# The parts of w_ada in a buffer of their own, and another order for the opening and block 0

## The chip, the cores and the metric

The kernel runs on one core of a Trainium2 chip. The metric is the device time of one execution in microseconds (us). Its engines are named as in the profile: PE (TensorE, matrix products), PEld (PE's weight loads), DVE (VectorE), ACT (ScalarE), POOL (GpSimd) and SP (SyncE, which here only issues DMAs). A name with q behind it (SPq, ACTq, DVEq, POOLq) is an engine's instruction queue.

## What is computed

One decoder block in float32 on 2048 rows of 1024 columns:

```
mod = silu(c) @ w_ada + b_ada ; sh1, sc1, g1, sh2, sc2, g2 = split(mod, 6)      # each 1024 wide
h   = rmsnorm(x, norm1_g) * (1 + sc1) + sh1
u_conv, u_ssm, gl_conv, gl_ssm = split(h @ w_in)                                # 1024, 512, 1024, 1024
y_conv = silu(layernorm(depthwise_conv31(a * sigmoid(gate)))) @ conv_proj
y_ssm  = gelu(diagonal state space scan of u_ssm) @ ssm_glu, halves za * sigmoid(zb)
x   = x + g1 * ((sigmoid(gl_conv) * y_conv + sigmoid(gl_ssm) * y_ssm) @ w_out)
h   = rmsnorm(x, norm2_g) * (1 + sc2) + sh2
x   = x + g2 * ((silu(f_gate) * f_up) @ w_ffn_out) ;  out = rmsnorm(x, final_g)
```

## The kernel before

**Products.** Each float32 operand of a large product is split into a high part and a low part in the float32r format, and a product is three matmuls (high by high, high weight by low data, low weight by high data: lines 1488 to 1490, and 1633 to 1635 for w_out).

**Stages.** An opening makes sh1 and sc1, the normalized first rows and the tables of the state space. Then four blocks (`mixers(b)`, b = 0 to 3) of 512 rows each run the mixers up to `x + g1 * ...`. The feed-forward follows. The change touches the opening and the four blocks; the feed-forward has the same work as before.

**Weight chunks.** In a block PE goes through 48 weight chunks of 128 x 1024 values: 4 of w_in for the state space (`us0` to `us3`), 8 for the convolution's inputs (`ua`, `ug`, in pairs), 16 for the gates (`gl0` to `gl15`), 8 of ssm_glu, 4 of conv_proj, 8 of w_out. SP loads a chunk into a ring of three buffers `raw` (`load`, L1871), POOL rounds it into `w_hi` (L1782) and subtracts for `w_lo` (L1784), each in a ring of two (SPL = 2), and PE takes 24 matmuls of 512 columns from it. So POOL may start chunk w when PE is through with chunk w-2. Every matmul waits in program order; the order of each engine is written out by hand, and each step of an engine raises a counting semaphore (`Steps`) on which the others wait.

**Parts of w_ada.** g1, sh2, sc2 and g2 are made one in each block (`MADE`). POOL forms `acc` = sum over k of `cact[:, k] * w_ada[k]`, k = 0 to 7, plus b_ada / 128 as a ninth part: nine loads of 128 x 1024 that go through the same ring `raw`, one behind every third weight chunk (`MIX_CHUNKS`). Each is a scaling (TENSOR_SCALAR, in place, L1761, or into `acc` for the first, L1768) and an addition (L1764), both 128 x 1024 (`part_of_ada`). PE sums `acc` over the partitions in `modulation` behind `cp1`.

**Opening.** sh1 and sc1 (2048 columns of w_ada) are made by PE from eight slabs of 128 x (4 x 512) values, 1 MB each, loaded by SP into four buffers `ada` (L1839); PE takes four matmuls with 4-column weights from each (L1434), in the order of the slabs, and only after `zc`, which DVE writes after the transpose `v0` of the poles' rows `nat_a` (L1423). DVE then writes `modrow` (L623), PE turns it (`mt`), DVE writes `scale0`, ACT makes h in eight tiles (two operations each, L1027) and DVE their low parts (`h_split`, L534), one behind each of the eight turns of three operations that write `wm` (L632 to L634). DVE's arithmetic for the state space (L586 to L619) stands ahead of `modrow`.

**Block 0.** It has work that the others don't: PE's transposes of `wm` and `cx` (`state_matrix`, L1467 and L1473) behind `us3`, whose results ACT copies back and stores to `wt_scratch`; the rotation tables (DVE `kargs` L523 to L526, ACT L1065 and L1066); DVE's 27 operations for `vm` behind `gated(0, 0)`; PE's `kernel_tiles` (L1482) behind `ug3`. ACT issues eight DMAs that gather `u8` (L1117) behind `state_matrix`, then the tables, then the sigmoids of `ug0` to `ug3` (L1121). From there on all blocks do the same: PE's `S0` to `S3` (L1543) on `u8`, DVE's rotation and scan (L745 to L777), the gates on PE meanwhile, `Y0` to `Y3`, the rest of the convolution on DVE (L711, 97 operations in one run), `ys_lo` (L534), for which PE waits ahead of `za0`. DVE's L799 to L803 give the sum that PE's `ln1` (L1571) takes.

**Places in memory.** `g2b` (128 x 1024) is written only in block 3, when g2 is ready. `acc` isn't used before block 0.

Of the kernel before, what the change touches and what calls it, by code (L numbers as in the profile page):

```python
# [7 lines left out]
ALU = mybir.AluOpType  # L8
# [6 lines left out]
P = 128  # L15
# [30 lines left out]
def build(nc, x, c, w_ada, b_ada, norm1_g, w_in, conv_w, conv_b, conv_ln_g, conv_ln_b, conv_proj,  # L46
# [8 lines left out]
    NB = SEQ // TB  # L55
# [13 lines left out]
    ADA = 4  # L69
# [61 lines left out]
    with ExitStack() as ctx:  # L131
# [116 lines left out]
        def early(at, end, *buffers):  # L248
# [21 lines left out]
        cact = vt[:, 6 * KD:7 * KD]  # L270

# [49 lines left out]
        pe_pro = ["v1", "v0"] + [f"ada{n}" for n in R(len(SLABS))] + ["mt"] + h_steps + ["v2"]  # L321
# [150 lines left out]
        zeros_in, ada_scaled = sem("zeros_in"), sem("ada_scaled")  # L472
# [20 lines left out]
        def _(dve):  # L493
# [88 lines left out]
            norm_scale("pro")  # L582

# [10 lines left out]
            link(v.reciprocal(den, den))  # L594
            link(v.tensor_tensor(t0, nr, ar, ALU.mult))
# [6 lines left out]
            link(v.tensor_tensor(qi, qi, den, ALU.mult))  # L602

            def by_h(a):
# [10 lines left out]
                                        op0=ALU.mult, op1=ALU.add))  # L615
            link(v.tensor_copy(bank[4][:], flat2(b1)))
# [4 lines left out]

# [366 lines left out]
        def _(act):  # L988
# [114 lines left out]
            def mixers(b, next_x, row, which, last=False):  # L1103
# [9 lines left out]
                if b == 0:  # L1113
                    state_matrix()
# [904 lines left out]
```

## Time and profile before

| | us |
|---|---|
| median of 3 runs (lowest, highest) | 2761.34 (2752.03, 2761.76) |
| the profiled execution's own time | 2760.32 |
| its span, first to last instruction | 2758.5 |
| PE busy in the span | 2609.3 |
| POOL busy | 1852.2 |
| DVE busy | 1472.9 |
| ACT busy | 722.2 |

The mean granted clock of TensorE is 0.972 of full speed. Block 0 begins on PE at 64.07 us, block 3 ends and the feed-forward begins near 1380 us. Busy shares are averages over stages with different limits; what a stage is limited by is read from the waits in it. Idle time of an engine off the chain costs nothing.

### The profile page before, as it was taken

Reading aid. Unit: us, or ns where it says so; the run is one execution under the profiler, and the core shown is the slowest. Engines: PE = TensorE matmul, PEld = TensorE weight load, DVE = VectorE, ACT = ScalarE, POOL = GpSimd, SP = SyncE. Lnnn points to the kernel's source line nnn. Section 1 sums busy time; section 2 is a strip of 40 time slices with the busy share of each in tenths; the row PEclk is TensorE's granted clock in tenths of the full one; section 3 lists DMA queues with packets and bytes.
Section 4 is the critical chain, followed back from the end, with each engine's and each line's share of the span. In section 5 each row is a group of like instructions: output and inputs, shape, how many; then the busy total and the mean of one; then the engine's idle time right before and its main releaser. Section 6 shows DMA issues by size and latency. Waiting matters only on the chain.

```text
span 2758.5 us, 30542 instructions
## 1 busy us (share of the span) xinstructions
PE 2609.3 (95%) x11671; PEld 2136.7 (77%) x11671; DVE 1472.9 (53%) x1766; ACT 722.2 (26%) x1118; POOL 1852.2 (67%) x1134
## 2 busy tenths in 40 slices
PE   5889899899989999899989999999999999999998
PEld 2678687777877788787778888878888877888886
DVE  5599743966269562894653333473333334645531
ACT  3212321024201430024333234542333321211100
POOL 1767556876666767766587776788777755666664
PEclk9999998999989999899999999999999999999999
DMA  8686337562574527564232333222322336655532
GB/s 238 149 212 186 104 126 173 153 188 95 162 188 123 177 84 210 148 187 141 85 111 73 92 92 115 88 73 85 92 75 86 91 134 221 186 182 188 172 126 76
DMA packets 422906, 378.28 MB, mean 137 GB/s; under 512 B 95641, under 2 KB 333929, under 8 KB 422633
## 3 DMA queue, kind: packets, MB, share of 16 engines
q1 hardware_dynamic: 316256, 299.48, 36.0%
q10 hardware_dynamic: 106504, 76.85, 10.0%
q8 instruction: 93, 1.52, 0.2%
q14 instruction: 53, 0.43, 0.0%
HBM read 312.11 MB, written 55.71 MB: 133 GB/s over the span
## 4 chain that ended last, share of the span: by engine, by line
PE 76%; DVE 8%; POOL 8%; DMA 4%; issue 1%; ACT 1%; ACTq 1%; DVEq 0%; POOLq 0%
PE bank L1488 16%; PE bank L1490 16%; PE bank L1489 16%; PE bank L1716 5%; PE bank L1717 5%; PE bank L1718 5%; POOL w_lo L1784 3%; DVE bank L711 2%; PE bank L1633 2%; PE bank L1635 2%; PE bank L1634 2%; POOL raw L1761 2%; PE bank L1543 2%; POOL w_hi L1782 1%; POOL acc L1764 1%
## 5 line engine op out<-in xcount | busy, mean ns | idle before, releaser
L1782 POOL CAST w_hi<-raw 128x1024 fp32r<-128x1024 f32 x192 | 215.5, 1122 | 474.1 <-PE bank L1490 360.0
L1784 POOL TENSOR_TENSOR w_lo<-raw,w_hi 128x1024 fp32r<-128x1024 f32 x192 | 481.5, 2508 | 15.4
L1488 PE MATMUL bank<-h_hi,w_hi 128*128 128x512 f32 x896 | 367.3, 410 | 64.9 <-POOL w_lo L1784 60.4
L1489 PE MATMUL bank<-h_lo,w_hi 128*128 128x512 f32 x896 | 360.3, 402 | 0.0
L1490 PE MATMUL bank<-h_hi,w_lo 128*128 128x512 f32 x896 | 359.2, 401 | 0.0
L711 DVE SCALAR_TENSOR_TENSOR bank<-uc,cwt,bank 128x512 f32<-128x512 f32 x464 | 328.4, 751 | 8.0
L1802 POOL TENSOR_TENSOR fw_lo<-fsum,fw_hi 128x512 fp32r<-128x512 f32 x176 | 233.7, 1330 | 106.2 <-ACT fw_hi L1296 106.2
L1488 PE MATMUL bank<-xc_hi_T,fw_hi 128*128 128x512 f32 x704 | 276.6, 393 | 8.6 <-DVE tr L895 6.3
L1716 PE MATMUL bank<-ow_hi,hid_hi 128*128 128x512 f32 x704 | 274.7, 390 | 7.6 <-DVE hid_lo L955 7.6
L1489 PE MATMUL bank<-xc_lo_T,fw_hi 128*128 128x512 f32 x704 | 275.1, 391 | 0.0
L1490 PE MATMUL bank<-xc_hi_T,fw_lo 128*128 128x512 f32 x704 | 275.1, 391 | 0.0
L1717 PE MATMUL bank<-ow_hi,hid_lo 128*128 128x512 f32 x704 | 274.5, 390 | 0.0
L1718 PE MATMUL bank<-ow_lo,hid_hi 128*128 128x512 f32 x704 | 274.4, 390 | 0.0
L1488 PEld LDWEIGHTS bank<-h_hi,w_hi 128*128 128x128 f32 x896 | 175.6, 196 | 111.9 <-POOL w_lo L1784 70.2
L1488 PE MATMUL bank<-xc_hi_B,fw_hi 128*128 128x512 f32 x528 | 207.7, 393 | 4.7 <-issue 2.9
L1490 PE MATMUL bank<-xc_hi_B,fw_lo 128*128 128x512 f32 x528 | 206.7, 392 | 0.0
L1489 PE MATMUL bank<-xc_lo_B,fw_hi 128*128 128x512 f32 x528 | 206.7, 391 | 0.0
L1490 PEld LDWEIGHTS bank<-h_hi,w_lo 128*128 128x128 f32 x896 | 175.3, 196 | 38.7
L1489 PEld LDWEIGHTS bank<-h_lo,w_hi 128*128 128x128 f32 x896 | 176.1, 197 | 35.9
L1802 POOL TENSOR_TENSOR fw_lo<-raw,fw_hi 128x512 fp32r<-128x512 f32 x110 | 151.0, 1373 | 60.6 <-ACT fw_hi L1296 60.6
L955 DVE TENSOR_TENSOR hid_lo<-hraw,hid_hi 128x512 fp32r<-128x512 f32 x88 | 142.3, 1654 | 92.0 <-ACT hid_hi L1384 92.0
L1830 POOL TENSOR_TENSOR ow_lo<-raw,ow_hi 128x1024 fp32r<-128x1024 f32 x66 | 168.6, 2555 | 5.3
(292 smaller groups left out, 5038.8 us busy)
## 6 DMA issues: line engine op xcount, KB each, us to landing
raw<-in_w_in SPq DMA_DIRECT2D x112, 512.0 KB, 4.2
raw<-in_w_ffn_in SPq DMA_DIRECT2D x66, 512.0 KB, 5.3
raw<-in_w_ffn_out SPq DMA_DIRECT2D x66, 512.0 KB, 4.3
hid_scratch<-tr SPq DMA_DIRECT2D x88, 256.0 KB, 2.8
hraw<-hid_scratch SPq DMA_DIRECT2D x88, 256.0 KB, 3.7
raw<-in_w_ada SPq DMA_DIRECT2D x32, 512.0 KB, 4.0
ssm_m<-vk_scratch SPq DMA_DIRECT2D x32, 512.0 KB, 5.6
raw<-in_ssm_glu SPq DMA_DIRECT2D x32, 512.0 KB, 3.5
```

The costliest lines, as they stand in the source:

```text
L711: ins = v.scalar_tensor_tensor(out=dst, in0=src, scalar=w, in1=conv_bank(m)[:], op0=ALU.mult, op1=ALU.add)
L955: v.tensor_tensor(hid_lo[n % RING][:], hraw[n % 4][:], hid_hi[n % RING][:].bitcast(F32), ALU.subtract).then_inc(hid_lo_done, 1)
L1488: t.matmul(dst, wh, xh, start=first, stop=False)
L1489: t.matmul(dst, wh, xl, start=False, stop=False)
L1490: return t.matmul(dst, wl, xh, start=False, stop=last)
L1716: t.matmul(dst, hid_hi[hs][:, cols], ow_hi[slot][:, wcols], start=(k == 0), stop=False)
L1717: t.matmul(dst, hid_lo[hs][:, cols], ow_hi[slot][:, wcols], start=False, stop=False)
L1718: ins = t.matmul(dst, hid_hi[hs][:, cols], ow_lo[slot][:, wcols], start=False, stop=(k == KF - 1))
L1782: g.tensor_copy(hi[:], src[:]).then_inc(hi_done, 1)
L1784: g.tensor_tensor(lo[:], src[:], hi[:].bitcast(F32), ALU.subtract).then_inc(split_done, 1)
L1802: g.tensor_tensor(fw_lo[i][:], part[WEIGHTS[i]], fw_hi[i][:].bitcast(F32), ALU.subtract)\
L1830: g.tensor_tensor(lo[:], src[:], hi[:].bitcast(F32), ALU.subtract).then_inc(ow_lo_done, 1)
```

## The change

1. **Parts of w_ada, their own buffer.** They leave the ring `raw` (`MIX_CHUNKS` is gone) and go to `ada_part`, which is the memory of `g2b`. SP issues part k just ahead of weight chunk 4k+2 of the block, after the last piece of part k-1.
2. **Four pieces.** The scaling is a TENSOR_TENSOR with a broadcast factor on 128 x 512, twice, then the addition on 128 x 512, twice. Part k has its pieces behind chunks 4k+1, 4k+2 (scaling) and 4k+3, 4k+4 (addition); part 0 is scaled straight into `acc`. So a piece stands behind chunks 1, 2 and 5 to 36. PE's `modulation` waits for the counters of the pieces.
3. **Opening.** DVE sums slabs 0 and 1 into `acc` (eight operations on 128 x 512), PE takes slabs 2 and 3, then the poles' transpose, then slabs 4 to 7, then one matmul that adds DVE's sum. `zc` is written before the poles. The rows x are issued by ACT behind the poles and log_dt. SP's slabs 4 and 5 wait for DVE, 6 and 7 for PE. DVE writes `modrow`, `mod`, `scale0` and h's low parts ahead of its state space arithmetic and between its parts, and `wm` behind them.
4. **Block 0.** PE and ACT take `ua0` and `ug0` ahead of `state_matrix`; ACT issues the gather of `u8` and the sigmoid of `ug0` ahead of its copies for `state_matrix`.

The core of the diff:

```diff
-        if w % 3 == 2 and w // 3 <= KD:
-            MIX_CHUNKS.append(("ada", w // 3))
+    NA, ADA_EVERY = KD + 1, 4
+        ada_part = g2b
 # pe_steps, block 0
-                names += [f"wt{n}" for n in R(8)] + ["ct0", "ct1"] ... conv_in(0, 1, 2, 3) ...
+                names += conv_in(0) + [f"wt{n}" for n in R(8)] + ["ct0", "ct1"] + conv_in(1, 2, 3)
-        pe_pro = ["v1", "v0"] + [f"ada{n}" for n in R(len(SLABS))] + ["mt"] + h_steps + ["v2"]
+        pe_pro = ["v1"] + slabs(2, 4) + ["v0"] + slabs(4, 8) + ["ada0", "mt"] + h_steps + ["v2"]
 # DVE, opening
+            link(v.tensor_copy(zc[:, :, 3], cact), "zc")
+            sums = acc[:, 0:HALF]
+            for rows in R(2):
+                dve.wait_ge(ada_in[rows], 16)
+                for j in R(KD // 2):
+                    k = rows * KD // 2 + j
+                    if k == 0:
+                        link(v.tensor_scalar(sums, ada[rows][:, j, :], cact[:, k:k + 1], None, ALU.mult))
+                    else:
+                        link(v.scalar_tensor_tensor(out=sums, in0=ada[rows][:, j, :], scalar=cact[:, k:k + 1], in1=sums,
+                                                    op0=ALU.mult, op1=ALU.add), f"slab{rows}" if j == 3 else None)
             dve.wait_ge(*tensor.after("pro", "v0"))
...
             norm_scale("pro")
+            dve.wait_ge(*tensor.after("pro", "ada0"))
+            link(v.tensor_copy(modrow[:], bank[7][0:4, :]), "modrow")
...
+            scale_of(0)
+            for k in R(2):
+                h_split("pro", k)
...
+            dve.wait_ge(*scal.after(0, "wt7"))
 # ACT, block 0
-                if b == 0:
-                    state_matrix()
                 act.wait_ge(uz_out, 64 * (b + 1))
...
                 if b == 0:
+                    sigmoid_u(0)
+                    state_matrix()
                     rotation_tables()
-                    for m in R(KC):
+                    for m in R(1, KC):
                         sigmoid_u(m)
 # PE, opening
+            modulation_rows(2, 4)
             pe.wait_ge(poles_in, 64)
             turn_rows_in(0, nat_a, bank[0])
+            modulation_rows(4, 8)
+            pe.wait_ge(pro_v, mark["slab1"])
+            t.matmul(bank[7][0:4, :], one_of_4[:], acc[:, 0:HALF], start=False, stop=True)
 # POOL
+            def scale_part(b, k, half, done):
+                cols = slice(half * HALF, (half + 1) * HALF)
+                factor = (cact[:, k:k + 1] if k < KD else part128[:]).broadcast_to([P, HALF])
+                dst = ada_part if k else acc
+                if half == 0:
+                    pool.wait_ge(part_in, 16 * (NA * b + k + 1))
...
+                g.tensor_tensor(dst[:, cols], ada_part[:, cols], factor, ALU.mult).then_inc(done, 1)
+            def add_part(b, k, half, done):
...
+                g.tensor_tensor(acc[:, cols], acc[:, cols], ada_part[:, cols], ALU.add).then_inc(done, 1)
...
+                    k, turn = divmod(w - 1, ADA_EVERY)
+                    if 0 <= k < NA and turn < 2:
+                        scale_part(b, k, turn, part_scaled)
+                    if 0 < k < NA and turn >= 2:
+                        add_part(b, k, turn - 2, (part_half, part_done)[turn - 2])
 # SP
+            def load_part(b, k):
+                if k == 1:
+                    sp.wait_ge(part_scaled, 2 * (NA * b + 1))
+                elif b or k:
+                    sp.wait_ge(part_half, KD * b + max(k - 1, 0))
+                    sp.wait_ge(part_done, KD * b + max(k - 1, 0))
...
+                    if n % ADA_EVERY == 2 and n // ADA_EVERY < NA:
+                        load_part(b, n // ADA_EVERY)
                     load(b, n, key)
```

## Rows read from the trace of the kernel before

**Rows 1.** The page's part 4: the chain that ended last, shares by engine.
```profile
PE 76%; DVE 8%; POOL 8%; DMA 4%; issue 1%; ACT 1%; ACTq 1%; DVEq 0%; POOLq 0%
```
**Rows 2.** PE's waits for POOL in blocks 1, 2, 3: us, times, longest.
```profile
PE bank L1488 <- POOL w_lo L1784: 14.8, 5, 6.3
...
PE bank L1488 <- POOL w_lo L1784: 14.8, 5, 5.3
...
PE bank L1488 <- POOL w_lo L1784: 15.1, 6, 5.3
```
**Rows 3.** Timeline of PE in block 1: start us, us, instruction, idle before, releaser.
```profile
444.18 0.50 PE L1488 MATMUL bank<-h_hi,w_hi 128*128 128x512 f32 x1 [1.54 <-POOL w_lo L1784]
...
458.14 13.50 PE L1543 MATMUL bank<-u,ssm_m 128*128 128x64 f32 x64 [2.79 <-DMA u<-us_scratch]
...
501.71 0.80 PE L1488 MATMUL bank<-h_hi,w_hi 128*128 128x512 f32 x1 [6.28 <-POOL w_lo L1784]
...
524.22 0.80 PE L1488 MATMUL bank<-h_hi,w_hi 128*128 128x512 f32 x1 [3.71 <-POOL w_lo L1784]
```
**Rows 4.** Windows: length, busy (x) of PE PEld DVE ACT POOL, PEclk, DMA share, GB/s.
```profile
520.00:530.00 10.00, 6.29 (x17) 4.61 (x16) 9.61 (x13) 0.60 (x1) 7.45 (x5) 0.67 0.46 134
...
590.00:600.00 10.00, 8.40 (x38) 6.63 (x37) 9.87 (x10) 8.10 (x9) 7.71 (x5) 1.00 0.71 230
```
**Rows 5.** Timeline of POOL in block 1.
```profile
488.17 4.67 POOL L1761 TENSOR_SCALAR raw<-raw,vt 128x1024 f32<-128x1024 f32 x1
...
496.49 1.98 POOL L1782 CAST w_hi<-raw 128x1024 fp32r<-128x1024 f32 x1
498.55 3.10 POOL L1784 TENSOR_TENSOR w_lo<-raw,w_hi 128x1024 fp32r<-128x1024 f32 x1
...
580.04 1.04 POOL L1782 CAST w_hi<-raw 128x1024 fp32r<-128x1024 f32 x1 [1.91 <-PE bank L1490]
581.16 2.40 POOL L1784 TENSOR_TENSOR w_lo<-raw,w_hi 128x1024 fp32r<-128x1024 f32 x1
583.54 2.85 POOL L1761 TENSOR_SCALAR raw<-raw,vt 128x1024 f32<-128x1024 f32 x1
```
**Rows 6.** One line, a half-width sum of the feed-forward: duration in ns min/median/max, times.
```profile
L1798 POOL TENSOR_TENSOR fsum<-raw,raw x22: 1289/1298/3223, 1388.5 to 2207.2; 128x512 f32<-128x512 f32 x22
```
**Rows 7.** DVE's waits between 570 and 640 us (block 1).
```profile
DVE yc L809 <- PE bank L1571: 22.8, 1, 22.8
```
**Rows 8.** DMA to landing (us, min/median/max) of all loads into `raw`.
```profile
DMA to landing us min/median/max: 3.3/3.8/12.5
```
**Rows 9.** Timeline of the opening, PE and DVE.
```profile
18.16 0.36 PE L1423 MATMUL bank<-ident,nat_a 64*128 64x64 f32 x1 [9.64 <-DMA nat_a<-in_ssm_a_im]
...
19.11 28.91 PE L1434 MATMUL bank<-ada,zc 128*4 128x512 f32 x64 [0.59 <-DVE zc L571]
...
48.13 0.68 DVE L623 COPY modrow<-bank 4x512 f32<-4x512 f32 x1 [3.99 <-PE bank L1434]
```
**Rows 10.** Windows of the opening and block 0.
```profile
10.00:15.00 5.00, 0.00 (x0) 0.00 (x0) 0.00 (x0) 1.74 (x3) 0.00 (x0) 1.00 1.04 403
...
34.00:44.20 10.20, 10.20 (x25) 2.09 (x24) 9.26 (x22) 0.12 (x1) 2.63 (x2) 1.00 1.06 307
...
48.10:72.30 24.20, 13.97 (x58) 10.43 (x58) 22.67 (x37) 11.00 (x16) 0.85 (x1) 0.72 0.47 132
...
94.20:123.60 29.40, 27.69 (x141) 22.83 (x140) 0.00 (x0) 11.27 (x13) 20.50 (x11) 1.00 0.91 184
...
168.00:287.00 119.00, 105.06 (x507) 86.92 (x505) 117.02 (x137) 22.44 (x31) 89.56 (x42) 0.96 0.68 188
```
**Rows 11.** Timeline of block 0: ACT, its queue, and PE.
```profile
97.36 1.09 ACT L1108 ACTIVATE uz<-bank 128x512 f32<-128x512 f32 x1 [11.32 <-PE bank L1490]
...
104.37 13.25 ACTq L1117 DMA_DIRECT2D u<-us_scratch  x8
...
289.58 0.80 PE L1488 MATMUL bank<-ys_hi,w_hi 128*128 128x512 f32 x1 [6.46 <-DVE ys_lo L534]
```

More of the change, by code:

```diff
@@ L304, in pe_steps @@
             if b == 0:
-                names += conv_in(0, 1, 2, 3) + [f"kk{n}" for n in R(8)] + quarters
+                names += conv_in(0) + [f"wt{n}" for n in R(8)] + ["ct0", "ct1"] + conv_in(1, 2, 3)
+                names += [f"kk{n}" for n in R(8)] + quarters
             else:
@@ L327, in act_steps @@
             if b == 0:
-                names += [f"wt{n}" for n in R(8)] + ["sk", "ck"] + [f"ug{m}" for m in R(KC)]
+                names += ["ug0"] + [f"wt{n}" for n in R(8)] + ["sk", "ck"] + [f"ug{m}" for m in R(1, KC)]
                 names += [f"kk{n}" for n in R(8)] + [f"S{q}" for q in R(NQ)]
@@ L602, in _ @@
             link(v.tensor_tensor(qi, qi, den, ALU.mult))
+            h_split("pro", 3)
             def by_h(a):
@@ L1426, in _, with modulation_rows @@
             turn_rows_in(1, nat_v, bank[1])
+            pe.wait_ge(pro_v, mark["zc"])
+            def modulation_rows(lo, hi):
+                for n in R(lo, hi):
+                    kind, half, rows = SLABS[n]
+                    pe.wait_ge(ada_in[n % ADA], 16 * (n // ADA + 1))
+                    for j in R(KD // 2):
+                        k, r = rows * KD // 2 + j, 2 * kind + half
+                        ins = t.matmul(bank[7][0:4, :], zc[:, k, 3 - r:7 - r], ada[n % ADA][:, j, :],
+                                       start=(n == 2 and j == 0), stop=False)
+                    ins.then_inc(*tensor.step("pro", f"ada{n}"))
+            modulation_rows(2, 4)
             pe.wait_ge(poles_in, 64)
             turn_rows_in(0, nat_a, bank[0])
-            pe.wait_ge(pro_v, mark["zc"])
-            for n, (kind, half, rows) in enumerate(SLABS):
-                pe.wait_ge(ada_in[n % ADA], 16 * (n // ADA + 1))
-                for j in R(KD // 2):
-                    k, r = rows * KD // 2 + j, 2 * kind + half
-                    ins = t.matmul(bank[7][0:4, :], zc[:, k, 3 - r:7 - r], ada[n % ADA][:, j, :],
-                                   start=(r == 0 and k == 0), stop=(r == 3 and k == KD - 1))
-                ins.then_inc(*tensor.step("pro", f"ada{n}"))
+            modulation_rows(4, 8)
+            pe.wait_ge(pro_v, mark["slab1"])
+            t.matmul(bank[7][0:4, :], one_of_4[:], acc[:, 0:HALF], start=False, stop=True)\
+                .then_inc(*tensor.step("pro", "ada0"))
             pe.wait_ge(pro_v, mark["modrow"])
@@ L1780, in _ @@
                         pool.wait_ge(*chunk_used[b - 1][NW - SPL + w])
-                    src, hi, lo = raw[n % RAW], w_hi[w % SPL], w_lo[w % SPL]
+                    src, hi, lo = raw[w % RAW], w_hi[w % SPL], w_lo[w % SPL]
                     g.tensor_copy(hi[:], src[:]).then_inc(hi_done, 1)
```

103 lines of the change are left out of this document (48 added, 55 removed).

## The prediction

> **What bounds the kernel now.** I read the chain first: three quarters of the span are PE, so what counts is where PE waits [rows 1]. Then PE's waits by block: in blocks 1, 2 and 3 nearly all are for POOL's `w_lo`, 14.8, 14.8 and 15.1 us [rows 2]. Then when they fall: in block 1 one of 1.54 ahead of a DMA wait, one of 6.28 and one of 3.71 around 500 to 525 us, and the rest, 14.8 - 1.54 - 6.28 - 3.71 = 3.3, in two of some 1.6 near 592 and 610 [rows 2, 3]. Then the clock: it is at full speed through the 1.6 us waits, and at 0.67 in the 10 us that hold the 3.7 us wait [rows 4]; TensorE's levels are 1.2 and 2.4 GHz, so the long waits cost more than their own length. Last POOL beside it: in quiet stretches a cast and a subtraction take 1.12 + 2.38 = 3.50 us start to start and POOL then waits 1.91 for PE, so PE's pace is 5.4 per chunk; beside DVE's rotation and scan the same pair takes 2.06 + 3.1 = 5.1 [rows 5]. A part of w_ada is a scaling of 2.85 plus an addition of some 2.4, 5.3 in all: more than the 1.9 that POOL has to spare, so each one ends as a PE wait of about 5.3 - 1.9 - 1.9 = 1.5, the seen 1.6 [rows 5].
>
> In the opening the transpose of the poles waits 9.64 us for its DMA, the slabs' matmuls start only then, and run 28.91 us without a gap; DVE waits for them with `modrow` [rows 9]. The slabs' data come at 403 GB/s meanwhile [rows 10], so PE, started late, sets this stretch.
>
> **Parts in four pieces, quiet stretches.** A piece is a 128 x 512 TENSOR_TENSOR. Its nearest row is a half-width sum on POOL, 1.30 us [rows 6]. A broadcast operand is not in the trace. Lower bound: 1.2, half of the full-width 2.4 [rows 5]; upper: 2.3, half of the slowest scaling, 4.67 [rows 5]. I take 1.3. Chunk and piece are 3.5 + 1.3 = 4.8, under 5.4: 0.6 to spare, and PE's waits behind a part go to zero: 3.3 us in block 1, the same in block 2. In block 3, with long waits of 5.3 [rows 2] and, like block 1's second, some 3.5, 15.1 - 1.5 - 5.3 - 3.5 = 4.8.
>
> The 1.54 us wait goes too but brings nothing: the next thing PE does is wait 2.79 for the gather of `u8` [rows 3], whose start hangs on `us3`, not on what lies between; that wait becomes 4.3.
>
> At one place page and rows differ. POOL's two-input multiplication replaces a one-input one; the one-input scaling is 2.85 us, the two-input subtraction 2.40 [rows 5], so the exchange costs nothing here. The Trainium skill, GPSIMD Engine Reference, section "Elementwise - side-by-side cycle accounting", has it the other way: bodies held by one port at 1.03 cycles per element, two-input ones near 2.6, at 1.2 GHz 0.88 and 2.2 us for 1024 elements as an estimate. By that, scaling would get dearer by 1.3 us per part and the piece would be 1.1 us; POOL would still fit into PE's pace, so the sum is the same by both.
>
> **The same beside DVE.** From chunk 11 to chunk 15 of block 1 POOL works beside rotation and scan. Each of its operations is there some 0.8 longer than in quiet (1.98 against 1.04, 3.10 against 2.40, [rows 5]). A chunk with a piece is then 5.1 + 1.3 + 0.8 = 7.2 against PE's 5.4: POOL stays the bound, but evenly. Step by step: chunk 11 starts at 485.3 and its piece ends at 491.0; chunk 12 is ready at 496.1, 13 at 503.3, 14 at 510.5, 15 at 517.0. PE, at 5.4 each, would wait 0.6, 1.8, 1.8 and 1.0 = 5.2 instead of 6.28 + 3.71 = 10.0: 4.8 saved. The clock: the second long wait lost 10 x 0.33 = 3.3 us [rows 4], the first about as much; if waits under 2 us leave the clock up, as in the second row of [rows 4], up to 6.5 more. I take half, 3.2. So 8.0, and 8.0 + 3.3 = 11.3 per block; rounded 11, 11 and 8.0 + 4.8 = 12.5: **34.5 us in blocks 1 to 3**.
>
> What is late next there: `ys_lo`. DVE waits 22.8 for PE's `ln1` [rows 7], of which PE needs some 5.4 for `za0`, `za1`, so there is room for 17 us: enough. `modulation` moves from a sum finished behind chunk 26 to one behind chunk 36, the chunk of `cp0`, `cp1`: the last piece ends 1.3 us behind the split and PE still has 5.4 of matmuls in front: nothing.
>
> **Loads.** Part k is issued behind the last piece of part k-1 (behind chunk 4k) and is wanted behind chunk 4k+1: 5.4 - 1.3 = 4.1 us later; loads land in 3.8 (median), 3.3 at best [rows 8]. Behind it on SP stands raw chunk 4k+2, due at 5.4 + 1.9 = 7.3 behind chunk 4k's split, issued at 1.7 and landing, with the part ahead of it (0.5 MB at 403 GB/s is 1.3), at 1.7 + 3.8 + 1.3 = 6.8. Both fit by half a microsecond. A late part holds POOL's next cast; POOL is a ready chunk ahead (1.9 us), so up to 2.4 late costs PE nothing once, and later pieces give back 0.6 each. Zero; if each of seven tight parts cost 1 us, 7 x 4 = 28.
>
> **Opening.** `zc` is ready at about 11 instead of 19. Slabs arrive at 403 GB/s shared with the 2 MB of x: four slabs and x are 6.3 MB, 15.6 us plus 2 to start: slab 3 at 17.6, slab 2 near 14. A slab is 28.91 / 8 = 3.6 on PE [rows 9]. PE: 2 and 3 from 14 to 21.2, the poles 0.4, four more slabs 14.4 to 36.0, the added matmul 0.9: 37 instead of 48. **11 us.** DVE's eight operations (0.7 each, as the 32 of half width in a busy time of 22.67 [rows 10], 6 in all) end near 17, slab 5 is issued there, in time. `modrow` then starts a stretch that took 24.2 us to h's last low part, of which 24 turns of `wm` at 0.70 were 16.8 [rows 10]. These move behind, and the state space arithmetic, about 10.0 [rows 10], moves in; with some 2 us of waiting for ACT's first two tiles it is 7.4 + 10.0 + 2 = 19.4: **5 us more.** `us0` ends near 57 instead of 73, `us3`, without POOL's waits beside the tables (5.1 and 0.4), near 73.6; ACT took it up at 97.36 before [rows 11].
>
> **Block 0.** Then `ua0`, `ug0`, with POOL beside DVE's tables now, 12 us: 85.5. `state_matrix` comes next, but its copies stand on ACT behind the gather of `u8`: ACT has `us3` at 73.6, the store's landing at most 7.0 later [rows 11], eight issues of 13.25 in all [rows 11], a sigmoid with its table 2: 96. PE gets its two first banks in and then **waits some 9 us for ACT, a new wait**; `ua1` starts near 102. Before, it would be 104.4 + 10.9 = 115. Gain 13; 4 more if the issues take 9 with less traffic beside them. The part-wait of 2.6 us ahead of `kernel_tiles` goes: 15 to 16. DVE, idle for 29.4 us before `gated(0, 0)` [rows 10], has `vm` done by 124 and is not late for `kernel_tiles` at 135.
>
> From the rotation on, DVE is the bound of block 0: 117 of 119 us busy from 168 to 287 [rows 10], and PE waits 6.46 for its `ys_lo` [rows 11]. This run moves as a whole with PE's `S3`. What POOL's pieces save PE in the gates is given back at `za0`, where the wait grows from 6.5 to some 14. So block 0 with its opening brings **15 us**, not 16 + 8 + 8.
>
> **Sum.** 15 + 34.5 = 49.5. The profiled execution took 2760.3 (span 2758.5, 1.8 around it), 1.0 below the median of the runs, 2761.3: 2760.3 - 49.5 = 2711.
>
> **Rivals.**
> A. As worked out: 2711. Chance 0.45.
> B. The stretch beside DVE gives nothing: four short operations meet DVE four times where two did, 8.2 us per part (4 x 2.05) against 6.1 to 8.3 before, and waits near 2 us pull the clock down as the 3.7 did. For it: the 0.8 per operation. Against: they are spread over four chunks. Only 3.3 + 3.3 + 4.8 = 11.4 and the opening's 15 remain: 2734. Chance 0.22. The Trainium skill, SBUF - State Buffer, section "SBUF: two separate sides", calls the pair of ports that both share an exclusive lock, under which the loser "fully blocks": that speaks for this rival, and the lengthened rows agree.
> C. More: waits below 2 us leave the clock up (another 3 x 3.3), the issues of `u8` are short (4) and DVE's run, meeting shorter POOL operations, shrinks by 2: 2711 - 16 = 2695. Chance 0.23.
> D. The gain at the front is eaten by ACT's gather or by DVE's fixed run, blocks 1 to 3 as in A with late loads: 2760 - 3 - 25 = 2732. Chance 0.06.
> E. Slower: the multiplication with a broadcast factor is dear. Scaling and adding pieces of mean p cost nothing until p passes 1.9 us; from there each of the 34 chunks with a piece adds p - 1.9 in four blocks. With 4.67 for the scaling piece, the mean is 3.0 and 1.1 x 34 x 4 = 150, less the 50: 2860. For it: no row shows the form. Against: POOL's other forms lie within 1.2 to 1.4 per half. Chance 0.04, with all other ways that end without gain.
>
> A run can tell 0.5% (14 us) from no change. Faster by over 0.5% 0.94, within 0.5% 0.03, slower 0.03. For 8 in 10 the range reaches over B and C: 2690 to 2741.
>
> **What would show it.** Right: no wait of PE for POOL near the former 592 and 610; four or so short ones near 495 to 520 with the clock up; a POOL multiplication of 1.3 us; `modrow` near 37; a wait of PE for ACT's `wm` copies of some 9 us; a wait for `ys_lo` in block 0 of over 10. Wrong: POOL waiting for `ada_part`'s DMA; pieces over 1.9; DVE's run from rotation to `ys_lo` in blocks 1 to 3 ending behind the gates; `us3` later than 80.

## Result, and the profile after

The changed kernel takes 2682.9 us (median of 4 runs, 2677.2 to 2688.2), against 2761.6 for the kernel before on the same chip: a ratio of 0.972 (95% interval 0.969 to 0.975). That is 79 us saved where the prediction had 49.5 and a range of 2690 to 2741. The profiled execution took 2686.0 us, with a span of 2684.2.

I set the two traces side by side at one mark in each block: the first matmul of the output product that waits. In blocks 0 to 2 it waits for `m_lo`; in block 3 the product's only wait is one for `w_lo`, some 30 us further on in it, which makes that stretch longer by as much in both kernels. The marks lie at 363.87, 687.98, 1012.59 and 1373.07 us before, and at 351.26, 651.62, 953.66 and 1302.45 after.

| stretch | before | after | gain | forecast |
|---|---|---|---|---|
| opening and block 0 | 363.9 | 351.3 | 12.6 | 15 |
| block 1 | 324.1 | 300.4 | 23.7 | 11 |
| block 2 | 324.6 | 302.0 | 22.6 | 11 |
| block 3 | 360.5 | 348.8 | 11.7 | 12.5 |
| the rest | 1385.4 | 1381.7 | 3.7 | 0 |

The gains add up to 74.4 us, the difference of the two profiled executions' spans; the medians differ by 79, so some 4 us of the saving lie outside what the traces can place. The miss is one of blocks 1 and 2. The page's chain after, shares of the span by engine, shows POOL at half of its share in [rows 1]:

```profile
PE 74%; DVE 13%; POOL 4%; DMA 3%; issue 2%; ACTq 2%; ACT 1%; SPq 0%; DVEq 0%; POOLq 0%
```

The timeline of PE in block 1 of the kernel after (start, duration, instruction, idle before it and its releaser) has six waits for POOL, and none ahead of the 64 matmuls of 64 columns that follow the gather of `u8`, the S stage:

```profile
440.80 7.25 PE L1568 MATMUL bank<-u,ssm_m 128*128 128x64 f32 x64
...
465.25 0.50 PE L1512 MATMUL bank<-h_hi,w_hi 128*128 128x512 f32 x1 [0.77 <-POOL w_lo L1814]
...
472.49 0.50 PE L1512 MATMUL bank<-h_hi,w_hi 128*128 128x512 f32 x1 [1.51 <-POOL w_lo L1814]
...
479.82 0.50 PE L1512 MATMUL bank<-h_hi,w_hi 128*128 128x512 f32 x1 [1.60 <-POOL w_lo L1814]
...
486.78 0.50 PE L1512 MATMUL bank<-h_hi,w_hi 128*128 128x512 f32 x1 [1.22 <-POOL w_lo L1814]
...
493.73 0.50 PE L1512 MATMUL bank<-h_hi,w_hi 128*128 128x512 f32 x1 [1.22 <-POOL w_lo L1814]
...
592.06 0.50 PE L1512 MATMUL bank<-ys_hi,w_hi 128*128 128x512 f32 x1 [0.86 <-POOL w_lo L1814]
```

Before, this S stage took 13.50 us behind a wait of 2.79 [rows 3]; now it takes 7.25 and waits for nothing. The busy time of the engines by window (the first number behind the window is its length, then PE, PEld, DVE, ACT, POOL; then the granted clock, the DMA share and GB/s) gives the clock in it, and in the stretch beside DVE that holds five of the waits:

```profile
440.80:448.10 7.30, 7.30 (x66) 7.29 (x65) 7.01 (x11) 2.39 (x4) 4.44 (x3) 1.00 1.01 249
...
465.00:500.00 35.00, 29.20 (x123) 22.69 (x124) 34.58 (x28) 2.89 (x5) 34.60 (x17) 1.00 0.51 125
```

The granted clock is 1.00 in both. The kernel before had 0.67 in the first of [rows 4], and this in its S stage, in the same view of its own trace:

```profile
458.00:471.70 13.70, 13.56 (x65) 13.56 (x66) 8.68 (x13) 1.81 (x4) 4.17 (x3) 0.52 0.55 130
```

The whole of block 1 of the kernel after, PE alone:

```profile
351.26:651.62 300.36, 292.42 (x1397) 1.00 0.58 163
```

The kernel before has 324.11 us here with PE busy 305.50 at a clock of 0.95. Of the 23.75 us, then, 10.7 are idle time (18.6 against 7.9) and 13.1 are busy time: the same 1397 matmuls at a higher clock.

Why the S stage does not wait is on ACT's and SP's queues. ACT after copies the last strip of `uz`, stores it, and issues the gather once the store has landed; SP has by then issued its four `ssm_m` loads (2 MB):

```profile
419.24 1.12 ACT L1123 ACTIVATE uz<-bank 128x512 f32<-128x512 f32 x1 [4.32 <-PE bank L1514]
420.39 0.33 ACTq L1127 DMA_DIRECT2D us_scratch<-uz  x1
424.89 6.58 ACTq L1130 DMA_DIRECT2D u<-us_scratch  x8
431.51 0.60 ACT L1134 ACTIVATE tr<-bank 128x512 f32<-128x512 f32 x1 [11.15 <-issue]
```

```profile
412.56 2.14 SPq L1938 DMA_DIRECT2D ssm_m<-wt_scratch  x4
417.45 11.24 SPq L1914 DMA_DIRECT2D raw<-in_w_in  x3
440.51 0.34 SPq L1900 DMA_DIRECT2D g2b<-in_w_ada  x1
```

The `ssm_m` loads go out 6.7 us ahead of the copy at 419.24, the store lands 4.5 us after its issue, the gather is issued in 6.6. The kernel before, SP's line first, then ACT's:

```profile
430.55 1.93 SPq L1895 DMA_DIRECT2D ssm_m<-wt_scratch  x4
```

```profile
431.80 1.12 ACT L1108 ACTIVATE uz<-bank 128x512 f32<-128x512 f32 x1 [4.32 <-PE bank L1490]
...
440.27 8.91 ACTq L1117 DMA_DIRECT2D u<-us_scratch  x8
```

There the loads went out 1.25 us ahead of the copy; the store took 7.3 and the issue of the gather 8.9. The parts no longer stand among the chunks in the ring of three, so SP runs about one chunk further ahead.

### The profile page after: what moved, and what is told of

Same layout as the page of the kernel before. It is cut to its first block, busy times and chain, and to the rows that moved or that the text cites. A ratio compares the mean times of both kernels' runs of the same rounds, so it can differ in the third digit from the quotient of the medians.

```text
span 2684.2 us, 30657 instructions
## 1 busy us (share of the span) xinstructions
PE 2568.9 (96%) x11657; PEld 2106.1 (78%) x11657; DVE 1511.2 (56%) x1774; ACT 724.5 (27%) x1120; POOL 1858.4 (69%) x1204
## 4 chain that ended last, share of the span: by engine, by line
PE 74%; DVE 13%; POOL 4%; DMA 3%; issue 2%; ACTq 2%; ACT 1%; SPq 0%; DVEq 0%; POOLq 0%
PE bank L1512 16%; PE bank L1513 16%; PE bank L1514 16%; PE bank L1742 6%; PE bank L1744 6%; PE bank L1743 6%; DVE bank L726 6%; PE bank L1659 2%; PE bank L1661 2%; PE bank L1660 2%; POOL w_lo L1814 2%; POOL w_hi L1812 1%; ACTq L1059 1%; DMA raw<-in_ssm_glu 1%; PE bank L1568 1%
## 5 line engine op out<-in xcount | busy, mean ns | idle before, releaser
L1814 POOL TENSOR_TENSOR w_lo<-raw,w_hi 128x1024 fp32r<-128x1024 f32 x192 | 487.5, 2539 | 15.4
L1812 POOL CAST w_hi<-raw 128x1024 fp32r<-128x1024 f32 x192 | 230.7, 1202 | 381.7 <-PE bank L1514 255.0
L1512 PE MATMUL bank<-h_hi,w_hi 128*128 128x512 f32 x896 | 357.0, 398 | 31.8 <-POOL w_lo L1814 26.8
L1514 PE MATMUL bank<-h_hi,w_lo 128*128 128x512 f32 x896 | 351.9, 393 | 0.0
L1513 PE MATMUL bank<-h_lo,w_hi 128*128 128x512 f32 x896 | 351.6, 392 | 0.0
L726 DVE SCALAR_TENSOR_TENSOR bank<-uc,cwt,bank 128x512 f32<-128x512 f32 x464 | 328.4, 751 | 8.0
L1512 PEld LDWEIGHTS bank<-h_hi,w_hi 128*128 128x128 f32 x896 | 170.2, 190 | 76.0 <-POOL w_lo L1814 35.9
L1514 PEld LDWEIGHTS bank<-h_hi,w_lo 128*128 128x128 f32 x896 | 169.8, 189 | 36.5
L1513 PEld LDWEIGHTS bank<-h_lo,w_hi 128*128 128x128 f32 x896 | 170.3, 190 | 34.3
L905 DVE TENSOR_TENSOR fsum<-bank,fcopy 128x512 f32<-128x512 f32 x44 | 30.4, 691 | 260.5 <-PE bank L1514 260.5
```

The source lines that it names most:

```text
L726: ins = v.scalar_tensor_tensor(out=dst, in0=src, scalar=w, in1=conv_bank(m)[:], op0=ALU.mult, op1=ALU.add)
L1512: t.matmul(dst, wh, xh, start=first, stop=False)
L1513: t.matmul(dst, wh, xl, start=False, stop=False)
L1514: return t.matmul(dst, wl, xh, start=False, stop=last)
L1812: g.tensor_copy(hi[:], src[:]).then_inc(hi_done, 1)
L1814: g.tensor_tensor(lo[:], src[:], hi[:].bitcast(F32), ALU.subtract).then_inc(split_done, 1)
```

## Experiments

One table for all, with the stretches of the profiled execution cut at the same marks ("rest" is from the fourth stretch's start to the span's end). "S stage" is block 1's: PE's wait for the gather, then the duration of the 64 matmuls. Runs are the lowest and highest. The kernels were run in four groups, in which the kernel before had medians of 2761.6, 2759.1, 2754.8 and 2758.5 us, so a few us between kernels of different groups say little. Nor is a profiled execution always like the median: that of `before_ssm6` is the fastest of its ten (2724.9 us), that of `whole_ssm8` the slowest of its ten (2756.8), and that of `front_only` 6.3 us above its median.

| kernel | us, runs | to mark 1 | block 1 | block 2 | rest | S stage |
|---|---|---|---|---|---|---|
| before | 2759.1 (2753.0-2774.6) | 363.9 | 324.1 | 324.6 | 1745.9 | 2.8 + 13.5 |
| after | 2682.9 (2677.2-2688.2) | 351.3 | 300.4 | 302.0 | 1730.5 | 0 + 7.3 |
| parts_only | 2694.9 (2693.2-2697.2) | 360.7 | 301.5 | 300.6 | 1731.2 | 0 + 7.3 |
| front_only | 2744.7 (2731.2-2757.2) | 344.9 | 325.6 | 323.1 | 1755.5 | 4.0 + 13.9 |
| before_ssm6 | 2733.9 (2724.9-2753.7) | 360.4 | 313.1 | 313.8 | 1735.8 | 0 + 7.4 |
| after_ssm8 | 2701.4 (2696.8-2703.0) | 352.2 | 308.2 | 307.4 | 1733.4 | 0 + 7.4 |
| whole | 2724.0 (2722.1-2724.8) | 350.4 | 316.5 | 317.9 | 1738.1 | 0 + 7.3 |
| whole_ssm8 | 2746.0 (2736.7-2756.8) | 354.3 | 330.5 | 328.4 | 1741.8 | 7.0 + 13.9 |
| raw_first | 2677.3 (2676.0-2680.2) | 346.4 | 299.9 | 303.5 | 1724.4 | 0 + 7.3 |
| bx_sp | 2677.4 (2671.9-2680.0) | 340.2 | 300.4 | 302.5 | 1727.0 | 0 + 7.3 |
| bx_sp_raw_first | 2671.4 (2667.5-2676.9) | 340.9 | 301.0 | 300.7 | 1732.6 | 0 + 7.3 |
| pieces_ts | 2687.6 (2682.3-2689.7) | 349.4 | 303.5 | 303.7 | 1729.0 | 0.2 + 7.4 |

**The two halves of the change apart.** `parts_only` is the kernel before with the parts' hunks alone:

```
-                if key[0] == "ada":
-                    part_of_ada(b, n, key[1])
+            k, turn = divmod(w - 1, ADA_EVERY)
+            if 0 <= k < NA and turn < 2:
+                scale_part(b, k, turn, part_scaled)
+            if 0 < k < NA and turn >= 2:
+                add_part(b, k, turn - 2, (part_half, part_done)[turn - 2])
```

> The kernel before with only the change to the parts of w_ada (own buffer, four pieces behind weight chunks); opening and block 0 in their old order. Theory 1: the parts bring what the traces show in blocks 1 to 3 (23.75 + 22.6 + 11.7 = 58 us), and nothing of the order is needed for it: 2761.5 - 58 = 2703, and up to 5 us less if the pieces help block 0 too; the sixty-four matmuls of 64 columns (the S stage of block 1) take 7.3 us at clock 1.00, where they took 13.5 us. Rival, the prediction on record: 34.5 us in blocks 1 to 3, so 2727, and the S stage still after a wait for the gather of u.

Measured 0.977 of before (0.975 to 0.980), 64 us, 8 more than expected, 3 beyond the margin given; theory 1 holds, the figure on record (2727) does not. Blocks 1 and 2 gain 22.6 and 24.0 us with the old opening, and block 0 gives 3.2.

`front_only` has the hunks of the opening and of block 0, with the parts whole in the ring; one line of them:

```
-        pe_pro = ["v1", "v0"] + [f"ada{n}" for n in R(len(SLABS))] + ["mt"] + h_steps + ["v2"]
+        pe_pro = ["v1"] + slabs(2, 4) + ["v0"] + slabs(4, 8) + ["ada0", "mt"] + h_steps + ["v2"]
```

> The kernel before with only the new order of the opening and of block 0 and two slabs summed by DVE; the parts of w_ada still go whole through the ring of four buffers. If the two halves of the change add up, it takes 2761.5 - 12.6 = 2749 (theory 1), with block 1 unchanged: a wait of 2.8 us for the gather and the S stage at 13.5 us. Rival: the whole parts in the ring hold up block 0's DVE-bound stretch once the rotation begins 13 us earlier, and little of the opening's gain reaches the end: 2755 to 2761.

Measured 0.9945 (0.992 to 0.997), 14 us; the rival is out. 64 + 14 = 78 against 79 for both: within the spread of the runs the halves add up. But not in each stretch: alone the new order is worth 19.0 us up to the first mark (363.9 to 344.9), on top of the parts in pieces 9.4 (360.7 to 351.3). Its S stage is as slow as before:

```profile
440.37 13.92 PE L1573 MATMUL bank<-u,ssm_m 128*128 128x64 f32 x64 [3.97 <-DMA u<-us_scratch]
```

**The ssm_m loads.** `before_ssm6` changes one number of the kernel before, and thereby issues the loads one chunk earlier:

```
-                ahead = {7: [0, 1, 2, 3], 14: [4, 5, 6, 7], 21: [8, 9], 22: [10, 11]}
+                ahead = {6: [0, 1, 2, 3], 14: [4, 5, 6, 7], 21: [8, 9], 22: [10, 11]}
```

> The kernel before with one number changed: in blocks 1 to 3 SP issues the four loads of ssm_m (2 MB) one weight chunk earlier (ahead of chunk 6 instead of 7). Theory 1: the wait for the gather of u and the slow S stage of the kernel before come from these 2 MB, which SP issued at 430.55, 1.2 us ahead of the copy of the last strip of uz, so that they lie beside the store (7.3 us to landing) and the gather (8.9 us). One chunk earlier they are gone by then: wait 0 to 1 us, S stage 7 to 9 us, 6 to 9 us per block in blocks 1 and 2, less in block 3: 2740 to 2748. Rival: the gather's time is its own, or the waits of 14.8 us for POOL set what is late, and the ssm_m loads do not matter: 2760 to 2763.

Measured 0.992 (0.989 to 0.994), 25 us, more than expected; in its profiled execution, 9 us below the median, blocks 1 and 2 each gain 11. SP issues the loads 5.9 us ahead of the copy of the last strip, and the gather is issued in 7.4:

```profile
422.53 2.10 SPq L1895 DMA_DIRECT2D ssm_m<-wt_scratch  x4
```

```profile
428.38 1.12 ACT L1108 ACTIVATE uz<-bank 128x512 f32<-128x512 f32 x1 [4.32 <-PE bank L1490]
...
434.81 7.40 ACTq L1117 DMA_DIRECT2D u<-us_scratch  x8
```

The S stage has no wait and takes 7.36. PE's wait of 1.54 us for POOL is still there, as are the long ones beside DVE (5.43 and 3.30), so the rival is out.

`after_ssm8` does the reverse to the kernel after (7 becomes 8).

> The kernel after with the same number changed the other way: the ssm_m loads of blocks 1 to 3 one weight chunk later (ahead of chunk 8), which lays them beside the store of uz and the gather of u again. Theory 1: the wait at the S stage comes back (2 to 4 us), the S stage takes 12 to 13.5 us again at about half the clock, and 8 to 11 us per block are lost in two or three blocks: 2700 to 2712. Rival: the S stage is fast since the short waits for POOL ahead of it are gone; then the time stays at 2681 to 2686.

The time came as theory 1 had it, 18.6 us lost; the place did not, and the sign that theory 1 named, a slow S stage, failed in all three blocks. The S stage is fast all the same. The loss is on the gather's other follower: ACT stands in the store's landing (7.7 us) and the gather's issue (8.1), and takes up `tr`, DVE's first input of the block, 17.0 us behind the copy of the last strip instead of 12.3. DVE starts 5.7 us later (437.82 against 432.15), is busy almost without a gap to the end of its run (130.1 of 132.0 us from the rotation to `ys_lo`), and PE waits for its last product, with a granted clock of 0.67 in the 5 us behind. ACT, then PE:

```profile
420.18 1.12 ACT L1123 ACTIVATE uz<-bank 128x512 f32<-128x512 f32 x1 [4.32 <-PE bank L1514]
421.33 0.33 ACTq L1127 DMA_DIRECT2D us_scratch<-uz  x1
429.05 8.10 ACTq L1130 DMA_DIRECT2D u<-us_scratch  x8
437.19 0.60 ACT L1134 ACTIVATE tr<-bank 128x512 f32<-128x512 f32 x1 [15.89 <-PE bank L1514]
```

```profile
586.93 0.77 PE L1512 MATMUL bank<-ys_hi,w_hi 128*128 128x512 f32 x1 [4.86 <-DVE ys_lo L533]
```

**Splitting against the buffer.** `whole` puts all of a part's pieces behind one chunk and leaves the rest of the kernel after as it is:

```
-                    if 0 <= k < NA and turn < 2:
-                        scale_part(b, k, turn, part_scaled)
-                    if 0 < k < NA and turn >= 2:
-                        add_part(b, k, turn - 2, (part_half, part_done)[turn - 2])
+                    if 0 <= k < NA and turn == 1:
+                        scale_part(b, k, 0, part_scaled)
+                        scale_part(b, k, 1, part_scaled)
+                        if k:
+                            add_part(b, k, 0, part_half)
+                            add_part(b, k, 1, part_done)
```

> The kernel after with all pieces of a part of w_ada behind one weight chunk (4k + 2) instead of one behind each of four: the part keeps its own buffer, loads and ssm_m loads stay where they are, only the split into four places is gone. Per part POOL works 2 x 1.04 + 2 x 1.29 = 4.7 us beside no DVE work, so a chunk with a part takes it 3.65 + 4.7 = 8.3 us. If the four places are what the change is worth (the prediction on record), the short waits of 1.5 us and the long ones of 6.28 and 3.71 us with the clock drop behind them return, 11 us per block in blocks 1 to 3: 2683 + 33 = 2716. If the buffer of its own is most of it (SP one chunk further ahead, the ssm_m loads clear of the store and the gather), the wait at the S stage stays away (S stage 7.3 us) and 2683 + 10 to 20 = 2693 to 2703.

41 us slower than after, 8 more than the larger of the two figures: both expected too little. The splitting is worth 16 us in each of blocks 1 and 2, the buffer keeps the S stage fast. In block 1 PE's waits of over 0.9 us are

```profile
471.88 0.80 PE L1512 MATMUL bank<-h_hi,w_hi 128*128 128x512 f32 x1 [7.16 <-POOL w_lo L1814]
...
501.32 0.79 PE L1512 MATMUL bank<-h_hi,w_hi 128*128 128x512 f32 x1 [5.82 <-POOL w_lo L1814]
...
587.46 0.50 PE L1512 MATMUL bank<-h_hi,w_hi 128*128 128x512 f32 x1 [2.85 <-POOL w_lo L1814]
```

and the first matmul behind the two long ones takes 0.80 us, not 0.50, as in [rows 3]: the granted clock is 0.50, the lower of its two levels, in the 3 us behind each. With one of 0.75 at 435.42 they make 16.6, against 7.2 after.

`whole_ssm8` does both: parts whole behind one chunk, and the loads one chunk later.

> The kernel after with both undone for blocks 1 to 3: all pieces of a part behind one weight chunk, and the ssm_m loads one chunk later. What is left of the change there is the buffer of its own. If a POOL wait ahead of the gather and the late ssm_m loads together make the wait for the gather and the slow S stage (one alone did neither: the kernel with the later loads alone and the one with the whole parts alone both had it at 7.3 us), the S stage goes back to 12 to 13.9 us in at least two blocks and the time to 2724 + 10 to 25 = 2734 to 2749. Rival: the part in the ring is what the S stage suffered from; then it stays at 7.3 us and the time is 2724 + 0 to 8.

2746.0 us, in the range of the first theory and 0.996 of before (0.994 to 0.998): nearly all of what the parts had brought is gone, and the wait for the gather and the slow S stage are back in all three blocks (12.3 to 13.9 us):

```profile
451.97 13.92 PE L1568 MATMUL bank<-u,ssm_m 128*128 128x64 f32 x64 [6.96 <-DMA u<-us_scratch]
```

So in block 1 it took two things to make the S stage late. The `ssm_m` loads beside the store put the gather off by some 4 us (in the four kernels with late loads its issue ends 17.0 to 17.8 us behind the last copy of `uz`, in the others 12.0 to 14.3). And the part and the three chunks that SP issues next have to fall on it: in `whole_ssm8` they go out at 435.85 and 439.24, with the gather's issue ending at 440.0; in `after_ssm8` SP issues nothing from 429.6 to 441.46, and the gather, issued until 437.15, has landed by 441.74. Counted from the last copy of `uz`, PE is ready for the S stage after 21.6 to 23.6 us in these kernels, and the gather has landed after 19.2 (`after`), 21.2 (`whole`), 21.5 (`after_ssm8`), 23.7 (`before_ssm6`), 26.3 (before) and 29.7 us (`whole_ssm8`): either thing alone leaves it in time or nearly so, both together do not. The second half of this is a reading of traces; no run moved those chunks alone. Nor are these the only way to a late gather: in block 3 of `bx_sp_raw_first` it is late with loads that go out 6.1 us ahead.

**Late chunks on SP.** In the kernel after POOL gets some chunks late (in block 3 it stands 4.86 us for a chunk of ssm_glu at 1197.49); PE's wait behind that one is its longest for POOL:

```profile
1201.34 0.80 PE L1512 MATMUL bank<-ys_hi,w_hi 128*128 128x512 f32 x1 [5.09 <-POOL w_lo L1814]
```

`raw_first` lets chunk 4k + 2 stand ahead of the part:

```
+                    load(b, n, key)
                     if n % ADA_EVERY == 2 and n // ADA_EVERY < NA:
                         load_part(b, n // ADA_EVERY)
-                    load(b, n, key)
```

> The kernel after, where SP issues the weight chunk of turn 4k + 2 ahead of the part of w_ada (in the kernel after the chunk stands behind the part, which waits until the part before has been added). If the chunks that POOL gets late (PE waits 3.51 us at 256.83 and 5.09 us at 1201.34) are late by their place on SP, both waits go, the one in block 0 perhaps for nothing since DVE's ys_lo is waited for later (8.13 us at 277.74), the one in block 3 with its cold start: 2674 to 2680. Rival: they are late since the transfers are slow in those stretches, or the part is late in their place: 2680 to 2686.

2677.3, in the range of the first. Its ratio to the kernel before in its own group, 0.972 (0.968 to 0.976), is no better than that of the kernel after, so the gain rests on the traces: both waits are gone, block 0 gained 4.9 us after all and block 3 7.7. In block 2 of this run the gather's issue took 10.1 us with one more chunk beside it, and PE waited 1.98 for it, but the S stage ran at full clock:

```profile
737.94 7.36 PE L1568 MATMUL bank<-u,ssm_m 128*128 128x64 f32 x64 [1.98 <-DMA u<-us_scratch]
```

In block 3 of the kernel before a wait of 1.85 stood ahead of an S stage of 12.83 us, with another wait of 1.54 for POOL 13 us ahead of it (in `whole_ssm8` one of 2.01, with one of 0.75 8 us ahead, and 12.26 us behind); here the 30 us ahead hold no other. So a wait's length alone does not say what the clock does.

**The opening.** The timeline of ACT after, ahead of the norm statistics:

```profile
12.57 0.73 ACTq L1059 DMA_DIRECT2D bx<-in_ssm_b_re  x1
13.33 19.27 ACTq L1059 DMA_DIRECT2D bx<-in_ssm_b_im  x2
32.63 4.70 ACTq L1059 DMA_DIRECT2D bx<-in_ssm_b_re  x1
37.38 1.06 ACT L1022 ACTIVATE junk<-xs 128x1024 bf16<-128x1024 f32 x1 [24.58 <-issue]
```

ACT stands 24.8 us in the issue of four loads in runs of 64 bytes, and the norm's statistics wait behind them. In the kernel before ACT issued the same four in 4.9 us, from 18.95 to 23.82, where the DMA engines moved 61 GB/s; here they moved 346. It is the change itself that put these issues into the stream of the slabs. `bx_sp` issues them on SP, behind its third chunk:

```
-                    act.dma_start(dst[rows, :, :], src[0].rearrange("g p h -> p g h")).then_inc(bx_in, 16)
...
             def load_small():
...
+                        sp.dma_start(dst[rows, :, :], src[0].rearrange("g p h -> p g h")).then_inc(bx_in, 16)
```

> The kernel after with the four loads of ssm_b (64-byte runs) on SP's queue behind its third weight chunk, instead of on ACT's ahead of the norm statistics. In the kernel after ACT stood in their issue from 12.57 to 37.3 us and modrow came at 46.49 instead of behind the last slab's matmul (39.2 us). If ACT's blocked queue is why the opening gained less than forecast: modrow at 40 to 41, first product of block 0 six us earlier, 2675 to 2678. Rival: block 0 is bound by DVE from its first strips on, or the loads come late for DVE on SP: 2681 to 2685, or above.

2677.4, as the first had it. `modrow` comes at 39.13 instead of 46.49:

```profile
39.13 0.68 DVE L593 COPY modrow<-bank 4x512 f32<-4x512 f32 x1 [5.92 <-PE bank L1455]
```

The first mark moves by 11.0 us, to 340.2; the medians differ by 5.5, within the spread of either kernel's runs.

Both edits (`bx_sp_raw_first`), and both again (`both_again`) beside the kernel after, repeated (`after_again`):

> Both edits at once (loads of ssm_b on SP; weight chunk ahead of the part). If both terms are real and apart from each other: 2667 to 2674, the fastest version. If either is hidden: 2675 to 2680.

> The version with the loads of ssm_b on SP and the weight chunk ahead of the part, again: 2671, within 5 us, and 8 to 15 us below the kernel after of the same call if its gain is real.

> The kernel after, unchanged, beside the version with both later edits on one chip: 2683, within 5 us.

2671.4 and again 2671.2 us (2664.4 to 2676.8), against 2685.3 (2680.8 to 2688.4) for the kernel after: 14 us less, no run of one within those of the other. This is the fastest version here, 0.968 of before (0.966 to 0.971). In block 3 both its profiles have the gather late again (waits of 3.7 and 3.8 us, S stages of 13.2 and 13.5), where `raw_first` alone waited 1.0 and `bx_sp` not at all; that is left to gain.

**The form of the scaling piece.** `pieces_ts` uses the operation with a per-partition scalar:

```
-                g.tensor_tensor(dst[:, cols], ada_part[:, cols], factor, ALU.mult).then_inc(done, 1)
+                g.tensor_scalar(dst[:, cols], ada_part[:, cols], factor, None, ALU.mult).then_inc(done, 1)
```

> The kernel after with the scaling pieces as an operation with a per-partition scalar (one tensor operand) instead of a multiplication by a factor broadcast along the row. By half of the rows of the kernel before (2.85 us quiet and 4.67 us beside DVE for 128x1024) a piece takes 1.4 us quiet and 2.3 us beside DVE, where the multiplication takes 1.04 and 1.9. Two pieces in five chunks beside DVE then cost PE 0.2 us each on average, less than 1 us per block: 2681 to 2686. If instead the form decides whether a piece is hidden, its wait grows by over 0.5 us and the clock falls: above 2690.

2687.6 us, 2.3 to 4.7 above the kernel after: at the edge of what can be told, and 1.6 above the range of the first; it is below that of the second. The two pieces beside DVE, minimum, median, maximum in ns:

```profile
L1794 POOL TENSOR_SCALAR g2b<-g2b,vt x2: 2404/2874/3345, 479.4 to 486.2; 128x512 f32<-128x512 f32 x2
```

## Why the prediction was wrong, step by step

**The step that failed** is the one on the gather: "The 1.54 us wait goes too but brings nothing: the next thing PE does is wait 2.79 for the gather of `u8`, whose start hangs on `us3`, not on what lies between; that wait becomes 4.3." The start did hang on `us3`, but through a store and a gather whose durations hang on what SP issues beside them, and taking the parts out of the ring moved SP's 2 MB by a chunk. The wait went to zero, and with it the lower clock of the S stage: 2.79 + 13.50 - 7.25 = 9.0 us, in block 1 and nearly so in block 2. `before_ssm6` shows that moving these loads alone does it: 0.14 + 7.36 us in block 1.

**The clock beside DVE** was sized at half ("I take half, 3.2"). Block 1's accounts: 23.75 = 9.0 at the S stage + 7.6 less waiting for POOL (14.8 to 7.2; forecast 3.3 + 4.8 = 8.1) + 7.1 that is left, all but 0.3 of it the clock elsewhere (the 0.3 is a wait for DVE). Of the 7.1 some 2 lie right behind the S stage, where the kernel before still had 0.85 over 13.3 us. The error is then 9.0 + (7.1 - 3.2) - 0.5 = 12.4, which is 23.7 - 11.3. Rival C had this half right: waits under 2 us do leave the clock up.

**Pieces** came as worked out or a little better. The kernel after's two forms between 360 and 440 us:

```profile
L1794 POOL TENSOR_TENSOR g2b<-g2b,vt x2: 1042/1042/1042, 422.8 to 428.2; 128x512 f32<-128x512 f32 x2
```

```profile
L1802 POOL TENSOR_TENSOR acc<-acc,g2b x2: 1291/1292/1292, 433.7 to 439.1; 128x512 f32<-128x512 f32 x2
```

1.04 and 1.29 where 1.3 was taken. The two-input multiplication by a broadcast factor is the cheapest of the three arithmetic forms seen; `pieces_ts`, the one-input form, takes 1.56. The Trainium skill, GPSIMD Engine Reference, section "Elementwise - side-by-side cycle accounting", has bodies bound by one port at 1.03 cycles per element and two-input ones at 2.6, 2.5 times as dear; these runs do not show that ratio. Beside DVE a chunk and its piece take POOL 7.2 us start to start, as forecast, and PE's waits are 0.77, 1.51, 1.60, 1.22, 1.22 for 0.6, 1.8, 1.8, 1.0:

```profile
476.57 3.20 POOL L1814 TENSOR_TENSOR w_lo<-raw,w_hi 128x1024 fp32r<-128x1024 f32 x1
479.74 1.89 POOL L1794 TENSOR_TENSOR g2b<-g2b,vt 128x512 f32<-128x512 f32 x1
481.57 1.94 POOL L1812 CAST w_hi<-raw 128x1024 fp32r<-128x1024 f32 x1
```

Rival B is out: the single operations are longer there, but spread over four chunks they leave waits below 2 us in block 1 (one of 2.2 in block 3) and the clock up. Rival E is out with the 1.04, and D with blocks 1 and 2; C named the right sign and too small a sum, since it too kept the wait for the gather, and its shorter run of DVE came out the other way (below).

**Quiet stretches.** Right: of the waits near 592 and 610 one of 0.86 is left.

**Loads at zero cost.** POOL waits for a part's DMA 12 times, 12.5 us in all, 2.6 at most; that was one of the signs of being wrong. In blocks 1 and 2 the one wait of PE behind it is that of 0.86. The zero was wrong in block 3. There one late chunk costs 5.09 us and a cold start, about what the S stage gives there (1.85 + 12.83 before, 0.79 + 7.36 after: 6.5); `raw_first` brings block 3 from 348.8 to 341.1 us. That 11.7 was measured for 12.5 forecast is two errors of opposite sign.

**Opening.** The slabs, the poles and the added matmul ran as worked out: PE was through them at 39.2 us (forecast 37). `modrow` at 37 failed, at 46.49, since the working left out ACT's own queue (24.8 us where the kernel before had 4.9; with these issues on SP it comes at 39.13). `us3` came at 85.54 for 73.6, past the 80 that was to show the prediction wrong: 9.5 us from `modrow`, and 2.4 on the way from there. The chain found most of this again behind: the "new wait of some 9 us for ACT" did not come, because ACT issued the gather in 5.3 us instead of 13.25 (88.72 to 94.0), and PE's waits for the `wm` copies are below 1 us. DVE's run starts at 155.06, 13 earlier, as forecast.

**Block 0 bound by DVE.** Right in kind. The run takes 120 us, and PE's wait at its end is 8.1, not 14:

```profile
277.74 0.79 PE L1512 MATMUL bank<-ys_hi,w_hi 128*128 128x512 f32 x1 [8.13 <-DVE ys_lo L533]
```

What the working had at nothing is that POOL's pieces take time from DVE. With the same 1774 instructions DVE is busy 1511.2 us in the kernel after and 1481.5 in `whole`; with its parts whole `front_only` has 1476.6, with spread pieces `raw_first` has 1510.7, and `pieces_ts`, whose scaling pieces have one tensor operand, 1494.9. Between `whole` and the kernel after 25 of the 30 us lie in blocks 1 to 3, where DVE's run was not what PE waited for, but for 1.0 us in block 2. What it costs block 0, where DVE is the bound, is not shown: the run is 120.1 us long after and 116.2 in `front_only`, but 117.3 in `raw_first` with its spread pieces, and 119.0 before against 116.2 in `before_ssm6`, whose block 0 is the same code. And of the 6.4 us between the first marks of `front_only` (344.9) and the kernel after (351.3) 4.9 go with the late chunk that `raw_first` mends. The Trainium skill, SBUF - State Buffer, section "SBUF: two separate sides", has the two engines share a lock; that operations of both are longer where they meet agrees with it.

The 3.7 us behind block 3 I cannot place; in the two kernels that were profiled twice this stretch differs by 1.2 and 2.1 us.

## What to carry to other kernels

An edit that frees a place in a shared ring moves every transfer behind it on that queue. Before pricing a wait for a DMA as fixed, list what the other queues issue from a chunk earlier to its landing, and who besides the waiting engine stands behind it: here the store and the gather held PE by its matmuls and DVE by ACT. Price a wait of a few microseconds with the matmuls behind it, at both levels of the clock, and take the two cases as two rivals, not their mean.

## What the runs showed of the hardware

- In blocks 1 to 3 of the fourteen profiles the S stage, 64 matmuls of 64 columns, took 7.25 to 7.4 us at a granted clock of 1.00 or 12.2 to 13.9 at 0.50 to 0.58, nothing between. Behind waits of 0 to 1.1 us they were always fast, behind 2.8 to 7.0 always slow; of three waits near 2, those of 1.85 and 2.01 were followed by the slow one, that of 1.98 by the fast.
- Kernels whose S stage is slow spread more from run to run: 26 us (`front_only`), 20 (`whole_ssm8`), 22 (before) against 2.6 (`whole`), 4 (`parts_only`) and 11 (after). `before_ssm6`, with a fast S stage and long waits left, spread 29. The wide ones have 10 to 19 runs and the narrow ones 4, which may account for much of it; no run shows that the S stage is the cause.
- POOL on 128 x 512 float32, quiet: multiplication by a broadcast factor 1.04 us, addition 1.29, scaling by a per-partition scalar 1.56; beside DVE's rotation 1.89, 2.15 and 2.4 to 3.3.
- Four loads of 128 KB in 64-byte runs held their issuing engine for 24.8 us while the DMA engines moved 346 GB/s, and for 4.9 us in the kernel before while they moved 61; on SP, behind the slabs, they were issued in 8.7 (31.91 to 40.6) beside 218.
- A store of 256 KB landed 6.9 to 8.5 us after its issue where 2 MB of loads had gone out on another queue 1.3 us ahead of the copy in front of it, and after 4.5 to 6.3 where they had gone out 5.9 to 6.7 us ahead (blocks 1 to 3 of all profiles).
- DVE pays for POOL's work beside it, by the form of that work: with the same 1774 instructions it was busy 1477 to 1484 us with the work on a part in one place, and with pieces in four places 1495 (one-operand scaling) or 1505 to 1524 (two-operand). Which property of the pieces it pays for is not shown.
